# Copies of the sampled caches: from four on ACT's queue in the prompt attention to 92 on GpSimd's in the projection stage

## The reference

```
h = x * (1 + scale_m) + shift_m                       # 544 tokens x 1024
P = h @ w_in                                          # 67 tiles of up to 128 columns
A, B, C = nsa(P), rwkv7(P), dilated(P)
x = LN(alpha * x + gate_m * (merge(A, B, C) @ w_o));  x = LN(alpha * x + gate_f * SwiGLU(...))
new['nsa_win'] = kvw_full[:, :, :, -n_pref_w:]        # a cache of n rows: n - 4 old ones, moved up
new['dil%d' % g] = kv_full[:, :, :, -n_pref:]         # by 4, then the 4 new rows
```

## Time and profile before

| | us |
|---|---|
| median of 3 timed runs (2625.4 to 2628.47) | 2626.2 |
| the profiled execution, device time | 2641.51 |
| its span | 2639.7 |
| PE busy | 2032.3 (77%) |
| DVE busy | 1271.1 (48%) |
| ACT busy | 520.9 (20%) |
| POOL busy | 270.6 (10%) |
| mean granted TensorE clock | 0.857 |

### The profile page before, as it was taken

One profiled execution on the slowest core, in us unless ns is written; L12 is line 12 of the kernel. 1 busy time (PEld: TensorE's weight loads), 2 busy tenths in 40 slices (PEclk: granted clock), 3 DMA queues, 4 the chain that ended last, 5 costly groups with the idle time before them and its releaser, 6 DMA issues. The chain is left out here.

```text
span 2639.7 us, 38466 instructions
## 1 busy us (share of the span) xinstructions
PE 2032.3 (77%) x16050; PEld 1728.5 (65%) x16050; DVE 1271.1 (48%) x2016; ACT 520.9 (20%) x1119; POOL 270.6 (10%) x282
## 2 busy tenths in 40 slices
PE   3995798798987897874449881167849939999995
PEld 2985787688887887872225551034348729999994
DVE  3124656765425576722216653546623274444445
ACT  1233333322222332212114440011101000000000
POOL 0000000000004222001114450031300000000000
PEclk7998899899997998965559985588979969999996
DMA  7445222122428666539991001253624013322320
GB/s 239 124 113 130 76 62 74 41 75 62 112 86 267 186 206 160 123 69 347 336 338 55 28 1 39 68 210 109 223 112 168 0 34 91 92 85 74 93 62 34
DMA packets 322362, 317.09 MB, mean 120 GB/s; under 512 B 124781, under 2 KB 278917, under 8 KB 317070
## 3 DMA queue, kind: packets, MB, share of 16 engines
q1 hardware_dynamic: 301486, 196.76, 25.6%
q0 software_dynamic: 18624, 67.64, 7.6%
q10 hardware_dynamic: 2080, 50.23, 5.5%
HBM read 287.10 MB, written 79.71 MB: 139 GB/s over the span
## 5 line engine op out<-in xcount | busy, mean ns | idle before, releaser
L307 PE MATMUL inp_acc<-hh,inp_wh 128*128 128x272 f32 (+1 forms) x1072 | 342.7, 320 | 32.7 <-DVE inp_wl L279 18.5
L307 PE MATMUL inp_acc<-hh,inp_wl 128*128 128x272 f32 (+1 forms) x1072 | 316.5, 295 | 0.0
L307 PE MATMUL inp_acc<-hl,inp_wh 128*128 128x272 f32 (+1 forms) x1072 | 316.0, 295 | 0.0
L307 PEld LDWEIGHTS inp_acc<-hh,inp_wh 128*128 128x128 f32 (+1 forms) x1072 | 207.8, 194 | 55.1 <-issue 27.9
L279 DVE TENSOR_TENSOR inp_wl<-inp_w,inp_wh 128x1024 fp32r<-128x1024 f32 (+1 forms) x67 | 81.2, 1212 | 269.3 <-ACT inp_wh L459 268.8
L307 PEld LDWEIGHTS inp_acc<-hl,inp_wh 128*128 128x128 f32 (+1 forms) x1072 | 208.5, 194 | 3.4 <-issue 3.0
L307 PEld LDWEIGHTS inp_acc<-hh,inp_wl 128*128 128x128 f32 (+1 forms) x1072 | 207.6, 194 | 0.5
L288 PE MATMUL ffn_acc<-ffn_hh,ffn_wh 128*128 128x272 f32 x704 | 146.9, 290 | 36.3 <-DVE ffn_wl L279 36.3
L1348 PE MATMUL cmp_pH<-cmp_RTh,cmp_w1h 128*128 128x256 f32 (+1 forms) x576 | 173.4, 301 | 0.3 <-DVE cmp_RTl L279 0.3
L1348 PE MATMUL cmp_pH<-cmp_RTl,cmp_w1h 128*128 128x256 f32 (+1 forms) x576 | 170.3, 296 | 0.0
L1348 PE MATMUL cmp_pH<-cmp_RTh,cmp_w1l 128*128 128x256 f32 (+1 forms) x576 | 170.0, 295 | 0.0
(11 more groups left out here) (446 smaller groups left out, 3953.8 us busy)
## 6 DMA issues: line engine op xcount, KB each, us to landing
inp_w<-in_w_in_dram SPq DMA_DIRECT2D x66, 512.0 KB, 4.4
out_dram<-in_cache_dil_dram ACTq DMA_DIRECT2D x1, 32704.0 KB, 161.8
ffn_w<-in_w_ffn_dram SPq DMA_DIRECT2D x60, 512.0 KB, 3.9
sdi_kv<-in_cache_dil_dram SPq DMA_DIRECT2D x192, 86.0 KB
pat_wada<-in_w_ada_dram SPq DMA_DIRECT2D x16, 1024.0 KB, 27.8
PT<-inp_o SPq DMA_DIRECT2D x58, 272.0 KB, 2.2
ada_wada<-in_w_ada_dram SPq DMA_DIRECT2D x8, 1024.0 KB, 9.2
out_dram<-in_cache_dil_dram ACTq DMA_DIRECT2D x1, 8128.0 KB, 51.3
```

The costliest lines, as they stand in the source:

```text
L307: i = pe.matmul(out, l, r, start=(first and n == 0), stop=(last and n == 2))
```

## The change

`shift_caches` becomes a part of `weave` on POOL in `project_and_mix`, and is gone from ACT in `prompt_attention`. `cache_pieces` cuts the same copies into 92: 64 of one row of the largest cache (511 KB each), 16 of four rows of the next (508 KB), 8 of four rows of the window cache (508 KB), 4 of sixteen rows of the smallest (496 KB). Piece i is issued when the tiles before number n = 15 + 50 i // 92 are done, so one or two go with each of tiles 15 to 64. `finish` waits for 92 copies instead of 4.

```diff
--- before.py
+++ after.py
@@ -546,16 +546,27 @@
 NEW_ROW_STORES = 3 + 6 + 9 * DB
 
 
-def shift_caches(sp, a, copied):
-
-    n = 0
-    for name, w, heads, cut in (("win", 512, 4, 4), ("dil0", 128, 8, 1), ("dil1", 512, 8, 4), ("dil2", 2048, 8, 28)):
+def cache_pieces(a):
+
+    pieces = []
+    for name, w, heads, rows, cut in (("dil2", 2048, 8, 1, 28), ("dil1", 512, 8, 4, 4), ("win", 512, 4, 4, 4), ("dil0", 128, 8, 16, 1)):
         src = a["cache_nsa_win" if name == "win" else f"cache_{name}"][0].rearrange("b v h t d -> (b v h) (t d)")
         dst = a[f"o_{name}_s"][0].rearrange("b v h t d -> (b v h) (t d)")
-        src, dst = src[:, DT * HD:], dst[:, 0:(w - DT) * HD]
-        sp.dma_start(dst.rearrange("r (c n) -> r c n", c=cut), src.rearrange("r (c n) -> r c n", c=cut)).then_inc(copied, 16)
-        n += 1
-    return n
+        for r in range(0, DB * heads, rows):
+            pieces.append(tuple(x.rearrange("r (c n) -> r c n", c=cut) for x in (
+                dst[r:r + rows, 0:(w - DT) * HD], src[r:r + rows, DT * HD:w * HD])))
+    return pieces
+
+
+def shift_caches(eng, proj, a, copied):
+
+    pieces = cache_pieces(a)
+    first, last = 15, len(proj.tiles) - 2
+    for i, (dst, src) in enumerate(pieces):
+        n = first + i * (last - first) // len(pieces)
+        yield proj.at(n)
+        eng.wait_ge(proj.done, 2 * n)
+        eng.dma_start(dst, src).then_inc(copied, 16)
 
 
 def head_sums(pe, out, ones, x, ready=None):
@@ -1237,7 +1248,7 @@
 
             @block.gpsimd
             def _(pool):
-                weave(mix.pool(pool))
+                weave(mix.pool(pool), shift_caches(pool, proj, a, m["copied"]))
 
 
 class Compression:
@@ -2098,7 +2109,6 @@
             @block.scalar
             def _(act):
                 act.wait_ge(loaded, NLOAD)
-                shift_caches(act, a, m["copied"])
                 nc.scalar.activation(qA[:, :, :], qA[:, :, :], ACT.Copy, scale=HD ** -0.5).then_inc(qs, 1)
                 nc.scalar.activation(qC[:, :, :], qC[:, :, :], ACT.Copy, scale=HD ** -0.5).then_inc(qs, 1)
                 for i in range(NU + 2):
@@ -2716,16 +2726,16 @@
             m["xT"] = mixer.enter_context(nc.sbuf_tensor("xT", [P, KD, NT], F32))
             merge(nc, a, m)
             feed_forward(nc, a, m)
-        finish(nc, m)
-
-
-def finish(nc, m):
+        finish(nc, a, m)
+
+
+def finish(nc, a, m):
 
     with nc.Block() as block:
 
         @block.sync
         def _(sp):
-            sp.wait_ge(m["copied"], 16 * 4)
+            sp.wait_ge(m["copied"], 16 * len(cache_pieces(a)))
             sp.wait_ge(m["token_rows_out"], 16 * NEW_ROW_STORES)
```

## The result

The changed kernel took 2559.0 us (median; 2549.2 to 2563.9) against 2627.0 us for the kernel before beside it: a ratio of 0.9737 (95% interval 0.9702 to 0.9771), 68 us less. Run again beside the kernel before, it gave 0.9738 (0.9716 to 0.9760). Forecast were 2557 us and a gain of 69.

What follows compares the result with a forecast made beforehand. The prompt attention was taken as bound by PE waiting for weight blocks starved by ACT's cache copies. Terms -67.3 - 2.7 - 6 + 7 = -69.0 us took 2626.2 us to 2557 us, range 2536 to 2602.

Steps and rivals of the forecast that it cites:

- The wait, -67.3 us: Prompt attention: all five PE waits for `pat_wada` weight blocks go, -67.3 us, bounds -60 to -67.3.
- The clock, -6 us: Prompt attention: PE runs partly at 2.4 instead of 1.2 GHz; a third of 18 us taken, -6 us.
- ACT's issue, -2.7 us: Start of the prompt attention: ACT no longer issues four copies ahead of its two scalings, -2.7 us.
- The projection, +7 us: Projection: the 92 added pieces delay other DMA at two places without slack, +7 us, bounds 0 to 20.
- The DQ stores at tile 19: Projection: two pieces set off by tile 17 delay the six `DQ` stores SP waits for, +3 us.
- The stores of the sample's state: Projection, 712.92 to 713.90 us: SP's wait for these stores now meets 4-row pieces, +4 us.
- ACT waiting for `inp_w`: Projection: ACT waiting for this weight load was listed as a sign that the forecast is wrong.
- GpSimd: Projection: 92 DMA instructions on idle POOL at 0.94 us each, 86 us, hidden because nothing waits for POOL there.
- (1): Projection tiles 50 to 62: all 4-row pieces fill the same four engines; 2610 us, chance 0.07.
- (2): Prompt attention: shorter first units keep the clock at 1.2 GHz longer, fifteen units lose time; +30 us, 2587 us, chance 0.08.
- (3): Whole projection: each piece delays one link by 1.5 us; 2690 us, decisive from 0.8 us per piece, chance 0.05.
- (4): Projection: DVE held up while POOL writes descriptors, 86 us if all on the path; 2636 us, chance 0.04.

Runs made afterwards that it cites:

- before, whole by GpSimd: Kernel before the change, with the four whole copies issued by GpSimd instead of ACT at the start of the prompt attention; ratio 0.9993 to the kernel before.
- the kernel with columns: Changed kernel with each of the 92 pieces a slice of columns of all rows, same tiles and bytes; ratio 0.9701 to the kernel before.
- in-attention run: Changed kernel with the 92 pieces issued by GpSimd in the prompt attention, two per unit, none in the projection; 2604.5 us, ratio 0.9863 to the kernel before.

## Why the prediction was right, and where it was off

Right are the mechanism and the sign of every term; that the median came within 2 us of the forecast is partly luck. The gain in the attention was forecast at 73.3 us with the clock, the cost in the projection at 7. The pair of profiles has 69.8 and 10.2, with ACT's 2.5 together 62 us; the medians have 68. The attention alone of one kernel differs by 10 us between two executions, so a hit within 2 us says little of the single terms. The forecast also took a profiled execution to be 15.3 us above the timed ones in both kernels. The changed kernel's was 4.9 above its median, so 2572.5 us for a profiled one was 9 us too long; since the sum was made of differences, the forecast of the median did not suffer.

**The wait, -67.3 us.** Right. All five waits went. The attention, over the nine executions whose kernels have no copy left in it, took 285.3 to 297.9 us, mean 293.1; before it took 365.8: -72.7, which is 67.3 of waits and 5.4 for the rest. The one block wait allowed for in the bounds did not come. Two edits that leave the copies in the stage and only cut and space them removed the waits as well, so what mattered is the standing queue of long copies, and not that the copies were there.

**The clock, -6 us.** The direction is right: in the first window the granted clock rose from 0.54 to 0.66. Up to the nineteenth unit the gain beyond the waits is 10 us (166.2 us before, 84.3 to 92.1 in the nine, mean 88.6), and 12 us against "before, whole by GpSimd", which has the same waits (170.2, of these 69.2). The term had a third of 18 us, and over half came. The 5.4 us of the whole stage look like the 6 by chance: the units behind the nineteenth took 195.1 to 207.5 us in the nine (mean 204.5), 199.6 before, but 207.6 with the copies issued by GpSimd, where all waits were there too. So these units scatter whatever the copies do, and nothing shows that the change gives time back there. A stage of one kernel differs by 10 us between two executions; the second kernel with the old copies would give 377.8 - 293.1 - 69.2 = 15.5 us in place of the 5.4.

**ACT's issue, -2.7 us.** Right: -2.5 us here, the scaling at this time of the changed kernel's ACT,

```profile
...
1223.17 1.91 ACT L2112 ACTIVATE pat_qA<-pat_qA 128x2048 f32<-128x2048 f32 x1 [41.92 <-DMA pat_distc<-in_c_distc_dram]
...
```

and -2.2 us when only the issuer was changed.

**The projection, +7 us.** Both places were named rightly, one was mis-sized. The DQ stores at tile 19: +3 expected, 2.2 and 3.6 found (against 69.8). The wait before was 23.6 us; the changed kernel has

```profile
...
ACT inp_tok L467 <- DMA TM<-inp_tok: 26.4, 1, 26.4
...
```

The stores of the sample's state: +4 expected, 8.0 and 7.6 found. The prediction added one late landing in front of a wait of SyncE, and counted on slack behind it. What came is that SyncE's issues were held as well: eight `OD` stores took 8.76 us to issue, before 4.41, and a `PT` store 6.45 us, before 0.3. The weight loads stood behind them, and ACT waited around tile 58, three times in these rows of its timeline:

```profile
...
734.75 1.06 ACT L459 ACTIVATE inp_wh<-inp_w 128x1024 fp32r<-128x1024 f32 x1 [10.35 <-DMA inp_w<-in_w_in_dram]
...
742.40 1.06 ACT L459 ACTIVATE inp_wh<-inp_w 128x1024 fp32r<-128x1024 f32 x1 [5.08 <-DMA inp_w<-in_w_in_dram]
...
746.27 1.06 ACT L459 ACTIVATE inp_wh<-inp_w 128x1024 fp32r<-128x1024 f32 x1 [0.92 <-DMA inp_w<-in_w_in_dram]
...
```

The text had listed "ACT waiting for `inp_w`" as a sign against the forecast; it came for these three blocks, worth the 8 us, and the last tile ended at 794.6 us, within the 15 us allowed. So the 4 us had the place right and the way wrong: the late landing costs nothing (the kernel with columns), the held issues cost 8. The term was 10.2 to 11.2 for 7, inside its bounds of 0 to 20.

**GpSimd.** 0.51 us for a piece, not 0.94: the row used was an indirect gather's, another kind of DMA. It cost nothing, since GpSimd was idle there. The in-attention run shows what it is worth where GpSimd is on the path: nearly all of it.

**The rivals.** (1) had the right shape and the wrong reach: a four-row piece is 8 records of 65,024 bytes and 2.5 us each, a single row 16 of 32,704 bytes and 1.5 us, and the former hurt; but only where a run of small stores met them (tiles 50 to 57 took their old time). Its condition, that all four-row pieces fall on the same four DMA engines, did not hold for GpSimd: by the times of the records up to nine of them overlapped in the changed kernel. Where ACT issued them all at once, no more than four overlapped, though the rest stood queued, and the queue filled 21.3% of the engines, 3.4 of 16; SyncE's had four or five. So the issuer bears on how many engines the row pieces keep busy. (2) The units from the nineteenth on ran at a clock of 0.86 against 0.92 and took 207.4 against 199.6 us, in the rival's direction, but a quarter of its 30 us and within what one kernel differs by; "before, whole by GpSimd" had 0.86 and 207.6 us there with all waits in place, so it is not the change; the units before them ran faster, not slower. (3) The contention was local: 11 us over 92 pieces is 0.12 us each, far from 0.8. (4) DVE's 67 casts of the projection (`inp_wl`) took 1212 ns each, as before; not so.

## What to carry to other kernels

In this kernel a bulk copy was free, to some 8 us, beside a compute-bound stage, once it was handed out in small pieces, spaced at one to three for each tile, by an engine on which nothing waits there. Look for the places where the stage issues many small DMAs or waits for its own stores, and leave them out: here that was the whole remaining cost. Moving alone failed (1.018), and so did cutting alone, in one burst ahead of ACT's scaling (1.020). Cut and spaced, but issued by an engine on the path, gave half of the gain (0.986). Moving was not needed: cut and spaced in the old stage by an idle engine gave 0.973, the same as the changed kernel, and the best placing in the projection 0.969.

## What the runs showed of the hardware

- Two queues moved the same number of packets in the same time, 620 each in 120 us, and so 38.39 MB against 0.30 MB: the long packets took nearly all of the engines, and a 512 KB weight load took 147.6 us to land.
- An issuing DMA instruction can be held for long while its queue is served slowly: 108.34 us for one of SyncE beside whole copies, 6.45 us beside pieces, 0.3 undisturbed; and ACT's 92 issues of 0.5 MB in one go took 129 us. The length of the issuing rows in a timeline shows it, the waits do not.
- GpSimd's queue and ACT's gave the same copy the same share: 81.6% of the engines in both, PE waiting 69.2 and 67.3 us.
- Pieces of one row of 511 KB were moved as 16 packets of 32,704 bytes, and rows of 127 KB as two of 65,024, in the shapes of the order rows (16x8176 and 2x16256 numbers of 4 bytes); the program's own cut of the 511 KB row into 28 is no longer in them.
- Four-row pieces issued by ACT in one go had at most four packets in flight at once, with GpSimd's up to nine.
- The selected attention took 203.5 to 206.0 us in the four kernels that ran on one chip and 189.9 to 191.4 in the eight on two others, whatever was done with the copies; the cause stays open.
